# Two transformer blocks of two layers each: three weight loads in two pieces, and TensorE's rows of a PEER layer as a loop

## What is computed

```python
# per chunk of 128 tokens; D = 1024, 8 heads, 2 x 128 sub-keys, top 16, 16384 experts
q = (xc @ w_q).reshape(c, PEER_HEADS, 2, PEER_HALF)
sc = jnp.einsum('chpd,hpnd->chpn', q, sub_keys)
top_s, top_i = lax.top_k(sc, PEER_TOPK)
# ... the best 16 of the 256 sums of a head give idx and gate (softmax)
u = u_tab[idx]
act = jax.nn.gelu(jnp.einsum('chkd,cd->chk', u, xc), approximate=False)
vsel = v_tab[idx]
return jnp.einsum('chk,chkd->cd', gate * act, vsel)
# and around it: x = layer_norm(ALPHA * h + peer_ffn(h, ...))
```

## Time and profile before

| | us |
|---|---|
| runs: median of 3 (lowest, highest) | 2226.44 (2225.19, 2228.56) |
| the profiled execution | 2224.23 |
| its span, first to last instruction | 2222.4 |
| TensorE busy in it | 1921.6 (86%) |
| DVE, POOL, ACT busy in it | 1430.5, 1202.6, 946.1 |
| bytes moved | 700.22 MB, mean 315 GB/s |

### The profile page before, as it was taken

How to read it: one execution, slowest core, us unless ns; L and a number is a source line. 1 busy time by engine, 2 the same in 40 slices (tenths; PEclk the granted TensorE clock), 3 DMA queues, 4 the chain that set the end, 5 groups by cost and what they waited for, 6 DMA issues and landing times.

```text
span 2222.4 us, 26832 instructions
## 1 busy us (share of the span) xinstructions
PE 1921.6 (86%) x8560; PEld 1263.7 (57%) x8560; DVE 1430.5 (64%) x3203; ACT 946.1 (43%) x2288; POOL 1202.6 (54%) x807
## 2 busy tenths in 40 slices
PE   8999999999999888888777777898898887777776
PEld 7889998889998655443223222397554442232222
DVE  7454227553227878776777766578787767767665
ACT  6644446644436543433334333366434333333332
POOL 6758876768883256676444444131565663443441
PEclk9999999999999999999999999999899999999999
DMA  6536655536656499999999999764999999999997
GB/s 195 160 110 195 190 169 176 152 123 191 192 171 229 155 397 414 421 422 421 422 421 422 421 422 421 312 242 152 374 418 420 422 421 421 422 422 421 422 421 301
DMA packets 119152, 700.22 MB, mean 315 GB/s; under 512 B 14464, under 2 KB 14464, under 8 KB 52992
## 3 DMA queue, kind: packets, MB, share of 16 engines
q0 software_dynamic: 73728, 536.90, 58.4%
q1 hardware_dynamic: 44752, 161.95, 22.8%
q10 hardware_dynamic: 560, 0.01, 0.0%
HBM read 697.77 MB, written 1.05 MB: 314 GB/s over the span
## 4 chain that ended last, share of the span: by engine, by line
PE 45%; DMA 36%; DVE 9%; ACT 4%; POOL 4%; issue 3%; SPq 0%; POOLq 0%; DVEq 0%; ACTq 0%
PE ps L715 44%; DMA arena<-in_table,arena 20%; DMA late_row<-in_table,arena 12%; DMA row_sb<-in_table,arena 3%; DVE arena L2647 2%; DVE late_row L2647 1%; POOL late_row L1455 1%; POOL w_split L1367 1%; POOL arena L1455 1%; ACT diag L1838 1%; DMA raw<-in_stream 1%; DVE arena L2284 1%; DVE w_split L2262 1%; ACT w_split L1496 0%; ACT arena L1832 0%
## 5 line engine op out<-in xcount | busy, mean ns | idle before, releaser
L1367 POOL TENSOR_TENSOR w_split<-raw,w_split 128x1024 fp32r<-128x1024 f32 x224 | 549.1, 2461 | 298.9 <-ACT w_split L1496 159.0
L715 PE MATMUL ps<-late_row,diag 128*128 128x512 f32 x984 | 463.4, 610 | 126.2 <-ACT diag L1838 126.2
L715 PE MATMUL ps<-hT_both,w_split 128*128 128x256 f32 (+2 forms) x3968 | 508.7, 288 | 22.8 <-DVE hT_both L2347 17.6
L715 PEld LDWEIGHTS ps<-hT_both,w_split 128*128 128x128 f32 (+1 forms) x3968 | 492.9, 193 | 42.8 <-issue 33.3
L715 PE MATMUL ps<-arena,diag 128*128 128x512 f32 x904 | 423.6, 609 | 94.7 <-ACT diag L1838 94.7
L1455 POOL DMA_INDIRECT late_row<-in_table,arena x246 | 277.7, 1129 | 306.3 <-PE ps L715 265.6
L2647 DVE CUSTOM_DVE_ANT_0 late_row<-late_row,x_res 128x1024 f32<-128x1024 f32 x246 | 312.8, 1275 | 149.5 <-DMA late_row<-in_table,arena 145.8
L1455 POOL DMA_INDIRECT arena<-in_table,arena x226 | 256.0, 1133 | 272.5 <-PE ps L715 224.3
L715 PEld LDWEIGHTS ps<-late_row,diag 128*128 128x128 f32 x984 | 180.7, 192 | 390.7 <-ACT diag L1838 207.0
L2647 DVE CUSTOM_DVE_ANT_0 arena<-arena,x_res 128x1024 f32<-128x1024 f32 x226 | 288.6, 1287 | 150.1 <-DMA arena<-in_table,arena 148.4
L1496 ACT ACTIVATE w_split<-raw 128x1024 fp32r<-128x1024 f32 x260 | 272.6, 1057 | 215.7 <-DMA raw<-in_stream 200.9
(11 more groups left out here) (300 smaller groups left out, 1738.5 us busy)
## 6 DMA issues: line engine op xcount, KB each, us to landing
raw<-in_stream SPq DMA_DIRECT2D x266, 512.0 KB, 4.3
distances<-in_stream SPq DMA_DIRECT2D x14, 512.0 KB, 4.7
row_sb<-in_row SPq DMA_DIRECT2D x2, 2048.0 KB, 12.7
late_row<-in_table,arena POOLq DMA_INDIRECT x246, 30.8
arena<-in_table,arena POOLq DMA_INDIRECT x226, 30.9
arena<-in_sub SPq DMA_DIRECT2D x2, 1024.0 KB, 7.7
arena<-in_stream SPq DMA_DIRECT2D x4, 512.0 KB, 5.0
late_row<-in_stream SPq DMA_DIRECT2D x4, 512.0 KB, 4.1
```

Source lines behind the costliest of these rows:

```text
L715: ins = nc.tensor.matmul(o, lhsT, rhs, start=start, stop=stop)
L1367: pool.tensor_tensor(w_lo[pair], raws_at[RAW_HOME[at] if narrow == N2_NARROW else at % raws], w_hi[pair].bitcast(F32), ALU.subtract).then_ ...
```

## The change

The last three weight chunks of a layer of the second block (39, 40, 41) are loaded by two DMAs each, one of partitions 0 to 119 and one of partitions 120 to 127; ACT's waits count 32 for such a chunk (`RAW_LANDED`). TensorE's rows 129 to 248 become a register loop of eight laps of fifteen rows; rows 128 and 249 to 255 stay straight code. Since a loop's body must name the same buffers in each lap, the diagonals of the rows from 129 on use five of the eight buffers in turn (15 is a multiple of 5), and row 128 a sixth; ACT waits for the row that last used the buffer (`DIAG_BEFORE`). The residual of tile 1 is added after row 128, ahead of the loop, instead of after row 201.

```diff
@@ -69,6 +69,11 @@
 BATCH_ROWS = [range(n, n + BATCH) for n in range(0, ROWS - SINGLES, BATCH)] + [range(n, n + 1) for n in range(ROWS - SINGLES, ROWS)]
 BATCHES = len(BATCH_ROWS)
 DIAGS = 8
+LAP_ROWS = 15
+LAPS_FROM, LAPS = TILE_ROWS + 1, 8
+LAP_DIAGS = 5
+DIAG_OF = [n % DIAGS if n < TILE_ROWS else LAP_DIAGS if n < LAPS_FROM else (n - LAPS_FROM) % LAP_DIAGS for n in range(ROWS)]
+DIAG_BEFORE = [max((m for m in range(n) if DIAG_OF[m] == DIAG_OF[n]), default=None) for n in range(ROWS)]
 
 
 N2_QUERY = N2_MIX + 8
@@ -87,7 +92,9 @@
 LAST_PARK = N2_NARROW + PARKS - 1
 LOADS2 = (*range(EARLY, N2_NARROW), LAST_PARK - 1, *range(LAST_PARK + 1, LAST_PARK + 4), N2_NARROW, N2_NARROW + 1,
           LAST_PARK + 4, LAST_PARK + 5, LAST_PARK, *range(LAST_PARK + 6, N2))
-NTH_RAW = [RAW_HOME[:c].count(RAW_HOME[c]) for c in range(N2)]
+WHOLE = ((0, P),)
+PIECES = {c: ((0, 120), (120, P)) for c in range(N2 - 3, N2)}
+RAW_LANDED = [16 * sum(len(PIECES.get(k, WHOLE)) for k in range(c + 1) if RAW_HOME[k] == RAW_HOME[c]) for c in range(N2)]
 RAW_BEFORE = [max((k for k in range(c) if RAW_HOME[k] == RAW_HOME[c]), default=None) for c in range(N2)]
 PARK_FREE = N2_MIX + 8
 FIRST_LAP = (0, 1, 2, 3, 4, 5, 7, 8, 9, 0, 1, 2, 3, 4, 5, 6)
@@ -96,7 +103,7 @@
 SELECT_AT = {0: 0, 1: 0, 2: 3, 3: 3}
 SELECT_AT.update({b: 1 for u in range(2, UNITS) for b in range(u * UNIT_BATCHES - 12 + 2 * (u == 2), u * UNIT_BATCHES - 6 + 2 * (u == 2))})
 ALL_SLOTS_FROM = 100
-OWN_ROWS_AT = (50, 100)
+OWN_ROWS_AT = 50
 
 
 ROW1 = dict(ret_g=64, dq_g=64, dk_g=64, diff_g=128, lq=128, lk=128, dec=16, lam_init=1, out_scale=1)
@@ -587,6 +594,10 @@
             def load(c, slot):
                 sp.dma_start(raws_at[slot], stream[c]).then_inc(w_ready[slot], 16)
 
+            def load_pieces(c, slot, pieces):
+                for first_part, end in pieces:
+                    sp.dma_start(raws_at[slot][first_part:end], stream[c, first_part:end]).then_inc(w_ready[slot], 16)
+
             def load_layer1(base, n, slots, params, following):
 
                 for dst, src in params:
@@ -622,7 +633,7 @@
                         sp.wait_ge(w_used, PARK_FREE)
                     if c == RAW2 - 1:
                         sp.wait_ge(mask_ready, MASKS)
-                    load(base + c, RAW_HOME[c])
+                    load_pieces(base + c, RAW_HOME[c], PIECES.get(c, WHOLE))
                     if c in LOADS_AT:
                         for dst, src, landed in others[LOADS_AT.index(c)]:
                             sp.dma_start(dst, src).then_inc(landed, 16)
@@ -1236,15 +1247,18 @@
                             w.mm(b[:, at:at + NK], pqT[:, h % 2, k, t * P:(t + 1) * P], sub_sb[:, 2 * h + k, :],
                                  True, True, bank_full if t and k else None)
 
+                def weighted_row(n, earlier=0):
+                    t, first_row, last_row = n // TILE_ROWS, n % TILE_ROWS == 0, n % TILE_ROWS == TILE_ROWS - 1
+                    pe.wait_ge(diag_ready, earlier + (n + 1))
+                    for c in range(2):
+                        very_last = n == ROWS - 1 and c == 0
+                        signal = row_used if very_last else None if c == 0 else out_full if last_row else row_used
+                        w.mm(acc[2 * t + c], diag[:, DIAG_OF[n], :], slots[slot_of[n]][:, D + c * 512:D + (c + 1) * 512],
+                             first_row, last_row, signal)
+
                 def weighted_rows(b):
                     for n in BATCH_ROWS[b]:
-                        t, first_row, last_row = n // TILE_ROWS, n % TILE_ROWS == 0, n % TILE_ROWS == TILE_ROWS - 1
-                        pe.wait_ge(diag_ready, n + 1)
-                        for c in range(2):
-                            very_last = n == ROWS - 1 and c == 0
-                            signal = row_used if very_last else None if c == 0 else out_full if last_row else row_used
-                            w.mm(acc[2 * t + c], diag[:, n % DIAGS, :], slots[slot_of[n]][:, D + c * 512:D + (c + 1) * 512],
-                                 first_row, last_row, signal)
+                        weighted_row(n)
 
                 query_part(open_bank(pe, B, "q0a0")[:, 0:2 * P], 0, 0, range(DT))
                 pe.wait_ge(sub_ready, 16)
@@ -1281,10 +1295,10 @@
                     for c in range(2):
                         w.mm(acc[2 * t + c], alpha_ident, x_res[:, t, c * 512:(c + 1) * 512], False, False)
 
-                for b in range(OPENING + 2, BATCHES):
+                for b in range(OPENING + 2, TILE_ROWS // BATCH):
                     weighted_rows(b)
-                    if b in OWN_ROWS_AT:
-                        own_rows(OWN_ROWS_AT.index(b))
+                    if b == OWN_ROWS_AT:
+                        own_rows(0)
                     for h in range(HEADS_FIRST, PH):
                         if b == UNIT_BATCHES * h - 17:
                             query(h, 0)
@@ -1292,7 +1306,15 @@
                             query(h, 1)
                         if b == UNIT_BATCHES * h - 14:
                             key_scores(h)
-                assert w.owed == 0
+                for n in range(TILE_ROWS, LAPS_FROM):
+                    weighted_row(n)
+                own_rows(1)
+                assert w.owed == 0 and LAP_ROWS == SLOTS
+                with pe.Fori(0, LAPS) as i:
+                    for k in range(LAP_ROWS):
+                        weighted_row(LAPS_FROM + k, i * LAP_ROWS)
+                for n in range(LAPS_FROM + LAPS * LAP_ROWS, ROWS):
+                    weighted_row(n)
 
             def keep_going(free, n):
 
@@ -1489,8 +1511,8 @@
 
                     in_block2 = self.narrow == N2_NARROW
                     slot = RAW_HOME[c] if in_block2 else c % self.raws
-                    nth = NTH_RAW[c] if in_block2 else c // self.raws
-                    act.wait_ge(w_ready[slot], i * (16 * step // self.raws) + 16 * (nth + 1))
+                    landed = RAW_LANDED[c] if in_block2 else 16 * (c // self.raws + 1)
+                    act.wait_ge(w_ready[slot], i * (16 * step // self.raws) + landed)
                     if c >= self.pairs and used_before(c, self.pairs, self.narrow) > 0:
                         act.wait_ge(w_used, i * step + used_before(c, self.pairs, self.narrow))
                     A(w_hi[pair_of(c, self.pairs, self.narrow)], raws_at[slot], ACT.Copy).then_inc(hi_ready, 1)
@@ -1833,9 +1855,9 @@
                           scale=gate[:, n // TOP, n % TOP:n % TOP + 1]).then_inc(acts_gated, 1)
                     for n in BATCH_ROWS[b]:
                         act.wait_ge(acts_gated, n + 1)
-                        if n >= DIAGS:
-                            act.wait_ge(row_used, rows_done(n - DIAGS))
-                        A(diag[:, n % DIAGS, :], ident[:], ACT.Copy, scale=acts[:, n:n + 1]).then_inc(diag_ready, 1)
+                        if DIAG_BEFORE[n] is not None:
+                            act.wait_ge(row_used, rows_done(DIAG_BEFORE[n]))
+                        A(diag[:, DIAG_OF[n], :], ident[:], ACT.Copy, scale=acts[:, n:n + 1]).then_inc(diag_ready, 1)
 
                 query_high_part(2, 0)
                 diags_of(0)
```

## The result

The changed kernel took **2241.97 us** (median of 6 runs, 2236.09 to 2243.64), beside 2225.82 us before (6 runs, 2224.23 to 2228.56): ratio 1.0065, with a 95% interval of 1.005 to 1.008. It is slower by 16 us; 2222.3 us was predicted, 2227.8 at most. The profiled execution took 2242.71 us with a span of 2240.9.

The account below looks back on a forecast made before the run. It took the slowest DMA engine of the gathers as the bound: lone tails of 2.4 + 2.2 us, less 2 x 0.25, gave 4.1 us off the 2226.44 us median, so 2222.3 us; eight in ten 2220.0 to 2227.8.

Parts of the forecast that it names:

- What bounds the kernel now: Both gather stages: DMA-bound at 421 GB/s, ended by the slowest engine, alone for 2.4 us in layer 1 and 2.2 us in layer 2.
- The pieces: Last three chunks as 120 and 8 partitions: one engine freed of 3.9 us per layer, eight carrying 0.49 us more.
- The freed engine is the last: End of both layers' gathers: the engine relieved of the chunks is the lone last one, gain 3.6 to 4.6 us.
- rival A: The forecast itself: the engine freed of the chunks ends the gathers; gain 3.6 to 4.6 us, 2221.8 to 2222.8; chance 0.52.
- The loop: TensorE's rows in laps: about four code fetches fewer per layer, zero on the path, the laps themselves costing nothing.
- C: Rival: TensorE's code fetches sit on the last engine, so the loop alone pays, 2221.8 to 2222.8 us; chance 0.08.
- D: Rival: each of eight laps fetches the loop's block again on the last engine; 2234.4 to 2240.0 us; chance 0.04.
- Five diagonals: ACT's diagonals in five buffers: the slot needed is free 5.8 us ahead, so cost nothing.
- the residual: Tile 1's four matmul passes, 2 us, moved from row 201 to 128: taken by the slack of two batches.
- The sum: Whole kernel: 2.4 + 2.2 = 4.6 us, less 2 x 0.25, a gain of 4.1 us, so 2222.3 us.

## Why the prediction was wrong

**What bounds the kernel now** held: the gathers' rate set the time, and what took from it was paid almost in full (with the pieces alone (36 + 18 + 36 + 16) x 50 = 5.3 MB are missing in the four stretches, 12.6 us, and 12.8 were measured).

**The pieces** is the step that failed. It charged a chunk's pieces their bytes at the known rate, 0.16 us a partition, and asked only which of sixteen engines has them. That the engines stay independent of each other was taken over from whole chunks, the only loads that the trace of before shows beside gathers, and no bound was set against it. Halves of 64 neighbouring partitions lose 10.4 us, 120 and 8 lose 12.8, 112 and 16 lose 8.0; odd and even partitions and column halves lose nothing. So the cost is in which partitions of the chunk a DMA spans, and it falls on the other transfers that move at the time. Whether it arises where the partitions are written or where their rows are read isn't shown, since the two go together in every run that loses. For this the Trainium skill has a table (SBUF — State Buffer, Door 1: The DMA port swizzle): the ports repeat every 32 partitions and change at 64, so that partitions 0 to 63, or 64 to 127, reach eight of sixteen ports, and every second partition reaches all. The halves, the parts of 32 and the odd and even ones agree with it; no row here names a port. Of 120 and of 112 partitions the table alone doesn't say it, since either range reaches all sixteen. That the engines stand on the same ports at the same moment is my reading there and isn't shown, nor is why 112 and 16 cost less.

The rule of the Trainium skill (DMA: Bandwidth & Descriptors, Rules for kernel authors) that I had weighed against the edit speaks of two transfers to disjoint partition halves, and says that they serialize. I read it as "nothing gained". The run with the halves shows a loss of 10.4 us.

**The freed engine is the last** (rival A, 0.52) failed too. After the change the lone stretch at the end of layer 1 was longer:

```profile
1437.00:1438.00 1.00, 1.00 (x4) 0.49 (x3) 0.74 (x2) 0.20 (x1) 0.00 (x0) 1.00 0.06 25
...
1440.00:1441.00 1.00, 1.00 (x3) 0.19 (x1) 0.24 (x2) 0.67 (x3) 0.00 (x0) 1.00 0.06 25
```

Four of these in place of two. At the end of layer 2, and with the pieces alone, no lone stretch is shorter than 2 us. More code for DVE moves the end in full, so the last engine is the one that carries DVE's code, and a split by partitions would have to spare that one. That this code alone makes it the last in the kernel before isn't shown. The prediction had this cause in hand (the ten q14 packets that "can hold one engine back steadily") and didn't use it.

**The loop** was right: 46 fetches in place of 53, and no time for them, since TensorE's fetches aren't on the last engine (C wrong) and no lap fetched again (D wrong). **Five diagonals** and **the residual** were right: in 1860 to 2180 us ACT waits for nothing before its diagonals, and TensorE keeps its slack (41.2 us of idle time before the matmuls on `late_row`, 41.4 before the change).

```profile
L1860 ACT ACTIVATE diag<-ident,arena 128x128 f32<-128x128 f32 x126 | 42.8, 386 | 0.0
...
L726 PE MATMUL ps<-late_row,diag 128*128 128x512 f32 x269 | 130.3, 626 | 41.2 <-ACT diag L1860 41.2
```

**The sum** had the right zeroes, and a gain of 4.6 us where a loss of 12.8 stood. Its range reached up only by known terms; the one way to more than 1 us of loss that I priced was the loop (D, 0.04). The whole change stands 3.3 us above the pieces alone; as the two intervals overlap and the change with odd and even partitions is back at 2226.08, I put that down to the scatter of executions. No version here beats the kernel before.

## What to carry to other kernels

Beside other transfers, don't split a DMA by ranges of neighbouring partitions: its own bytes are the smaller part of the price, the larger is what it takes from all others in flight. If a load must be split, by columns or by every second partition was free here. And ask for an untested shape of transfer what it does to the others' rate, and set a bound on the slower side, before the gain of a few tenths of a microsecond a chunk is added up.

## What was new about the hardware

- Six chunks of 0.5 MB in pieces of 120 and 8 partitions, in a stream at 421 GB/s, cost some 2 us each: the rate fell to 338 over 10 us, 277 at the lowest, at an unchanged busy share. Loads alone fell from 307 GB/s (275 at the least in the other kernels) to 224.
- Every second partition, 64 at a time, cost nothing that shows (ratio 1.0003, 0.9994 to 1.0012).
- Code fetches of DVE load the DMA engine that ends the gathers, in both layers: eight fetches more cost 9.3 us, eight of ACT's 2.1 us, which isn't clear of noise. Fewer DVE instructions in the gathers might therefore bring time; that wasn't tried.
